# The output projections with seven block products for eight

## The chip, the cores and the metric

One core of a Trainium2 chip runs one program. The metric is the device time of one execution in microseconds (us), lower is better. The kernel before was timed in three runs.

## The reference, cut to what matters

The reference runs a first block (a mixer of three branches and a feed-forward layer) and then two layers of a second block (attention and a recurrent branch side by side). Three places multiply a concatenated activation by a 1024 x 1024 output weight and add the gated product to the residual stream. All is fp32.

```python
# first block: called "one" here; x has 1024 tokens
y_lat = jnp.concatenate([hy_lat, gla_lat, gdn_lat], axis=-1) @ w_out
x = x + g1 * y
x = x + g2 * sq_relu_mlp(modulate(x, norm2_g[l], sh2, sc2), w_mlp1[l], w_mlp2[l])
...
# second block, l = 0 ("two0") and l = 1 ("two1")
out_x = jnp.concatenate([att_x, m_x], axis=-1) @ w_out
x = x + gate_x * out_x
if not last:                       # two0 alone: 256 more tokens
    out_c = jnp.concatenate([att_c, m_c], axis=-1) @ w_out
    ctx = ctx + gate_c * out_c
```

After "one" and "two0" comes a root-mean-square norm with scale and shift, whose result feeds the next matrix products. After "two1" comes the final norm and the output.

## The kernel before, in words

**Storage.** Activations lie channel-major: channel in the partition, tokens along the free dimension, 8 channel tiles of 128. `XT` is the residual stream, `cat` the concatenated activation, `hT0` (region `R1`) the normed stream. Token blocks (`BLKS`) are 512, 512 and 256 (context) tokens. Weights come through a ring of four 1 MB slots (`K.W`), each with 256 output channels of the weight, that is one pair of output tiles.

**Stages.** The program is a list of stages (`plan`), and each engine's instructions are written out stage by stage in that order. Semaphores order the engines; `begin` makes an engine wait for what every engine did last in the stage before. Within a stage each engine works its own list in order, so an instruction that waits holds all behind it.

**Output projection** (`OutProj`, line 3213, three instances). TensorE walks the blocks, in each of them the 8 output tiles, and in each tile 8 matmuls over the inner channel tiles (L3247) into one of six PSUM banks. An fp32 matmul of the program is two MATMUL records in the trace. For each tile VectorE adds gate times product to `XT` (L3268), ScalarE squares the sum (L718), GpSimd adds the squares up (L728). "one" and "two1" have two blocks, "two0" three.

**The norm that follows** (`Rms`, line 825; `Finish` in "two1") is cut into parts 0 to 7 for each block. In part 1 TensorE multiplies the sum of squares by the mean matrix (L735, L737). In part 2 ScalarE takes Ln (L902) out of bank 6 and Exp (L904), each with a load of its table. In parts 3 to 7 VectorE scales eight tiles (L888) and ScalarE shifts them (L908). The projection runs the parts of block i - 1 one by one behind the tiles of block i; the parts of the last block come after the projection. In `Finish` part 1 is a small mean product (L3635) and Ln and Exp (L3653, L3656); parts 2 to 5 transpose four token tiles each (L3644), of which the block 0 ones use banks 6 and 7 alone; VectorE and ScalarE scale them (L3675, L3661), GpSimd multiplies by the gain (L3688), and SyncE stores them (L3712).

**Around the projections.** In "one" the residual stream comes back from HBM by a 4 MB DMA that GpSimd issues when the stage before has ended (`RestoreX`, L3198); VectorE waits for it ahead of its first add. Then GpSimd fetches two tiles of the second block's context. Behind "one" TensorE works in this order: mean product of block 1, the transposes of those two context tiles into banks 4, 5, 7 and 6 (L779), and the feed-forward layer (L3423). In "two0" and "two1" the stream is fetched during attention (L4738), and all projection weights but the first slot wait until attention's last transposes. Behind "two0" TensorE begins with the gate rows of block 0 (L1095), each matmul of which waits for the normed tile it reads.

**Seven for eight, as the feed-forward layer has it** (`Mlp.seven`, L3376). A 2 x 2 by 2 x 2 block product is made of seven block products instead of eight, with four sums of weight quarters on GpSimd (L3499 to L3505) and sums of input quarters on VectorE (L3517 to L3523 for its first product). Three products accumulate in bank "a", which is read out in between:

```python
product(a, S2, T2, False).then_inc(P.sem, P.up(("mlp", "P16", a)))
pr.open(e, d)
product(d, S1, T1, True).then_inc(P.sem, P.up(("mlp", "P5", d)))
```

## Time and profile before

| what | value |
| --- | --- |
| runs | 3688.92, 3693.72 and 3693.81 us; median 3693.72 us |
| profiled execution | span 3689.8 us; its own time is not listed apart from the span |
| mean granted TensorE clock | 0.988 of full speed |
| TensorE matmul busy | 3569.2 us, 97% |
| VectorE, ScalarE, GpSimd busy | 47%, 26%, 17% |
| all three output projections (L3247) | 896 MATMUL records |

The span runs from the first to the last instruction of one profiled execution; the runs' times include what lies around it. Matmuls are pipelined, so a record's duration overlaps the next one; the step from one tile's end to the next is the time that counts. "issue" is time for which the profile shows nothing that was waited for. TensorE's granted clock has two levels, 1.2 and 2.4 GHz, given as 0.5 and 1.0; a window's figure is the mean over it.

### The profile page before, as it was taken

How to read it: one execution, taken by the hardware profiler on the slowest of the kernel's cores; microseconds unless marked ns; L12 is line 12 of the kernel's file. 1: busy time of each engine (PE TensorE's matmuls, PEld its weight loads, DVE VectorE, ACT ScalarE, POOL GpSimd, SP SyncE). 2: the span in 40 equal slices, each digit the busy share in tenths (PEclk: the TensorE clock that was granted, in tenths of full speed). 3: DMA queues.
4: the chain of work that ended last, by engine and by line, in shares of the span. 5: the costliest groups of instructions: out<-in, count | busy, mean ns of one | idle time of the engine just before them, and what ended most of it. 6: DMA issues, size and time to landing. Idle time of an engine off the chain costs nothing.

```text
span 3689.8 us, 48255 instructions
## 1 busy us (share of the span) xinstructions
PE 3569.2 (97%) x19396; PEld 2260.5 (61%) x19396; DVE 1726.9 (47%) x3669; ACT 972.1 (26%) x1822; POOL 629.7 (17%) x572
## 2 busy tenths in 40 slices
PE   6999999999989999999999999999999999999998
PEld 3578976754744444444444588867654568866654
DVE  3877873274752334344334836323531464523531
ACT  5224422222103100000015214313541312313531
POOL 4002220231001312222214013110001102211001
PEclk8999999999989999999999999999999999999999
DMA  6301130453351111111102214120020413210021
GB/s 203 143 10 35 38 112 19 147 198 107 135 187 46 46 35 45 46 46 46 46 25 90 93 61 113 33 72 12 1 92 0 173 36 94 79 61 24 1 86 46
DMA packets 190445, 266.05 MB, mean 72 GB/s; under 512 B 27309, under 2 KB 133400, under 8 KB 189584
## 3 DMA queue, kind: packets, MB, share of 16 engines
q1 hardware_dynamic: 176576, 194.70, 16.9%
q0 software_dynamic: 13648, 68.26, 4.9%
q8 instruction: 157, 2.57, 0.3%
q14 instruction: 64, 0.52, 0.0%
HBM read 228.11 MB, written 34.81 MB: 71 GB/s over the span
## 4 chain that ended last, share of the span: by engine, by line
PE 88%; DVE 5%; ACT 2%; issue 2%; DMA 1%; POOL 0%; POOLq 0%; SPq 0%; DVEq 0%; ACTq 0%
PE ps L3376 19%; PE ps L3247 9%; PE ps L1038 9%; PE ps L4338 7%; PE ps L1060 6%; PE ps L4631 4%; PE ps L4808 3%; PE ps L1125 2%; PE ps L4288 2%; PE ps L4865 2%; PE ps L4848 2%; PE ps L3444 1%; PE ps L2939 1%; PE ps L1817 1%; PE ps L1833 1%
## 5 line engine op out<-in xcount | busy, mean ns | idle before, releaser
L3376 PE MATMUL ps<-big 128*128 128x512 f32 x1624 | 697.1, 593 | 0.0
L3376 PEld LDWEIGHTS ps<-big 128*128 128x128 f32 x1624 | 309.1, 190 | 387.8 <-issue 384.7
L1038 PE MATMUL ps<-big 128*128 128x512 f32 (+1 forms) x1056 | 402.0, 541 | 0.0
L3247 PE MATMUL ps<-big 128*128 128x512 f32 (+1 forms) x896 | 361.0, 564 | 4.6 <-issue 2.6
L1038 PEld LDWEIGHTS ps<-big 128*128 128x128 f32 x1056 | 199.9, 190 | 195.9 <-issue 189.8
L3247 PEld LDWEIGHTS ps<-big 128*128 128x128 f32 x896 | 170.6, 191 | 190.0 <-issue 184.4
L3569 DVE SCALAR_TENSOR_TENSOR big<-ps,big 128x512 f32<-128x512 f32 x212 | 159.2, 751 | 242.6 <-PE ps L3376 208.6
L4338 PE MATMUL ps<-big 128*128 128x256 f32 x1152 | 252.6, 380 | 0.0
L4338 PEld LDWEIGHTS ps<-big 128*128 128x128 f32 x1152 | 217.6, 190 | 28.9 <-issue 0.7
L1060 PE MATMUL ps<-big 128*128 128x256 f32 (+1 forms) x1344 | 229.0, 333 | 0.0
L1060 PEld LDWEIGHTS ps<-big 128*128 128x128 f32 x1344 | 208.3, 191 | 21.9 <-ACT big L2342 2.5
L3268 DVE SCALAR_TENSOR_TENSOR big<-ps,big 128x512 f32<-128x512 f32 (+1 forms) x56 | 39.8, 712 | 315.1 <-PE ps L3247 295.1
L728 POOL TENSOR_TENSOR big<-big 128x512 f32<-128x512 f32 (+1 forms) x90 | 109.5, 1222 | 439.8 <-ACT big L718 437.8
L718 ACT ACTIVATE big<-big 128x512 f32<-128x512 f32 (+1 forms) x120 | 68.5, 594 | 393.4 <-DVE big L3268 312.0
L1207 DVE SCALAR_TENSOR_TENSOR big<-big 128x1024 f32<-128x1024 f32 x130 | 168.8, 1299 | 4.6
L4631 PE MATMUL ps<-big 128*128 128x512 f32 (+1 forms) x416 | 158.5, 544 | 1.9 <-DVE big L4522 1.9
L4959 DVE CUSTOM_DVE_ANT_0 big<-ps,big 128x512 f32<-128x512 f32 (+2 forms) x144 | 96.0, 705 | 133.6 <-PE ps L4836 127.4
L4808 PE MATMUL ps<-big 128*128 128x256 f32 x576 | 132.5, 384 | 0.0
L3559 DVE TENSOR_TENSOR big<-big,ps 128x512 f32<-128x512 f32 x45 | 30.8, 685 | 213.6 <-PE ps L3376 213.6
L1125 PE MATMUL ps<-big 128*128 128x512 f32 (+1 forms) x320 | 126.7, 553 | 3.0 <-ACT big L1185 2.0
L4631 PEld LDWEIGHTS ps<-big 128*128 128x128 f32 x416 | 79.0, 190 | 80.6 <-issue 75.9
L4808 PEld LDWEIGHTS ps<-big 128*128 128x128 f32 x576 | 106.7, 190 | 26.9 <-DVE big L4963 9.7
(516 smaller groups left out, 5245.6 us busy)
## 6 DMA issues: line engine op xcount, KB each, us to landing
big<-in_w_mlp SPq DMA_DIRECT2D x32, 1024.0 KB, 5.4
big<-in_w_in SPq DMA_DIRECT2D x29, 1024.0 KB, 5.6
big<-in_w_mod SPq DMA_DIRECT2D x24, 1024.0 KB, 7.4
big<-in_w_ada SPq DMA_DIRECT2D x24, 1024.0 KB, 5.6
big<-us_scratch SPq DMA_DIRECT2D x72, 256.0 KB, 4.5
hs_scratch<-big POOLq DMA_DIRECT2D x3, 5120.0 KB, 19.0
xs_scratch<-big POOLq DMA_DIRECT2D x16, 640.0 KB, 3.5
big<-hs_scratch POOLq DMA_DIRECT2D x9, 1024.0 KB, 8.1
```

Source lines behind the costliest of these rows:

```text
L728: e.tensor_tensor(self.acc[i], self.acc[i], self.sq[q % len(self.sq)][:, 0:n], ALU.add).then_inc(G.sem, G.up(("added", self.tag, q), ("sum ...
L1038: t = e.matmul(b[:, 0:n], wv[:, k, 128 * m:128 * m + 128], K.hT[:, k, t0:t0 + n], start=(k == 0), stop=(k == 7))
L1060: t = e.matmul(b[:, 0:nn], K.hT[:, k, 128 * i:128 * i + 128], wv[:, k, 0:nn], start=(k == 0), stop=(k == 7))
L1125: t = e.matmul(b[:, 0:n], wv[:, k, 128 * m:128 * m + 128], K.hT[:, k, t0:t0 + n], start=(k == 0), stop=(k == 7))
L1207: e.scalar_tensor_tensor(dlat, zlat[:, :, tap:tap + c.seg], c.wcol(m, tap), dlat, ALU.mult, ALU.add).then_inc(V.sem, V.up((self.tag, c.wha ...
L3247: t = e.matmul(b[:, 0:n], wv[:, k, c:c + 128], cat[:, k, t0:t0 + n], start=(k == 0), stop=(k == 7))
L3376: t = e.matmul(z, w[:, k, c], y, start=(first and k == 0), stop=(k == nk - 1), skip_group_check=not first)
L3569: e.scalar_tensor_tensor(x, self.bank(u)[:, :], self.gcol[:, c:c + 1], x, ALU.mult, ALU.add).then_inc(V.sem, V.up(*keys))
L4338: x = e.matmul(b[:, 256 * q:256 * q + 256], m.hT[:, k, 128 * t:128 * t + 128], wv[:, k, :], start=(k == 0), stop=(k == 7))
L4631: t = e.matmul(b[:, 0:n], wv[:, k, c:c + 128], K.hT[:, k, t0:t0 + n], start=(k == 0), stop=(k == 7))
L4808: t = e.matmul(b[:, 0:256], wv[:, k, 128 * (j % 2):128 * (j % 2) + 128], K.hT[:, k, 256 * p:256 * p + 256], start=(k == 0), stop=(k == 7))
L4959: e.tensor_tensor_reduce(S[c][:, c0:512], self.s.bank(u)[:, c0:512], m.wm[:, c0:512], 64 ** -0.5, (m.m0 if n < 7 else m.snk)[:, c:c + 1], ...
```

## The change

The 1024 x 1024 by 1024 x 1024 product is cut into pairs of output tiles. One pair is a 2 x 2 by 2 x 2 block product: 2 output tiles x 2 halves of the inner channels x 2 blocks of 512 tokens. It is now made with seven products of 4 matmuls each, 28 matmuls for 32. "two0" does this for all four pairs and then the 256 context tokens directly; "one" and "two1" do it for three pairs, and the last pair (tiles 6 and 7, both blocks) directly.

New work: four subtractions of 128 x 2048 on VectorE at each projection's start (`input_sums`), ahead of the wait for the residual stream and of the first add; four sums of 128 x 512 on GpSimd for each pair (`weight_sums`), those of two pairs ahead of the first sum of squares; and seven adds into `XT` for a pair instead of four (`seven_out`). The T sums lie in `R1`, the S sums in its end and in spare memory. The squares follow the new order of tiles (`made`). The norm's parts move: in "two0" the parts of blocks 0 and 1 both run behind the eight context tiles, n-th parts behind the n-th tile, with the mean products in banks 6 and 7; in "one" and "two1" parts 0 to 2 of block 0 run behind tile (block 1, 6) and parts 3 to 7 behind the last tile, (block 1, 7).

```diff
@@ -703,15 +703,17 @@
-    def __init__(self, K, tag, x, blks, at_ring, at_sums, ring=3, g=None):
+    def __init__(self, K, tag, x, blks, at_ring, at_sums, ring=3, g=None, order=None):
         self.at, self.mean = K.book.at, K.mean
+        order = [(i, k) for i in range(len(blks)) for k in range(8)] if order is None else order
+        self.number = {x: q for q, x in enumerate(x for x in order if 0 < x[1] < 7)}
         self.tag, self.x, self.blks, self.g = tag, x, blks, g
...
-        q, ring = 6 * i + k - 1, len(self.sq)
+        q, ring = self.number.get((i, k), 0), len(self.sq)
...
-        q, n = 6 * i + k - 1, self.blks[i][1]
+        q, n = self.number[i, k], self.blks[i][1]
         e.wait_ge(*self.at("square", self.tag, i, k))
         if k > 1:
-            e.wait_ge(*self.at("added", self.tag, q - 1))
+            e.wait_ge(*self.at("added", self.tag, self.number[i, k - 1]))
...
-    def __init__(self, K, tag, w, gates, blks, after, sums, post, away=None, held=None):
...
-        self.cat = K.big[:, K.M0:K.M0 + 8 * (TT if len(blks) == 3 or tag != "one" else T)]
+        n = TT if len(blks) == 3 or tag != "one" else T
+        self.cat = K.big[:, K.M0:K.M0 + 8 * n].rearrange("p (a b) -> p a b", a=8)
+        self.sevens = self.pairs(blks)
+        self.ts = [K.R1[:, 2048 * i:2048 * i + 2048].rearrange("p (k t) -> p k t", k=4) for i in range(4)]
+        self.ws = [[mem.get(512).rearrange("p (k c) -> p k c", k=4) for _ in range(4)] for _ in range(2)]
+
+    @staticmethod
+    def pairs(blks):
+
+        return 4 if len(blks) == 3 else 3
+
+    @classmethod
+    def rest(cls, blks):
+
+        if len(blks) == 3:
+            return [(2, j) for j in range(8)]
+        return [(i, j) for i in range(2) for j in range(2 * cls.pairs(blks), 8)]
+
+    @classmethod
+    def made(cls, blks):
+
+        return [(i, 2 * p + m) for p in range(cls.pairs(blks)) for m in range(2) for i in range(2)] + cls.rest(blks)
+
+    def parts(self, n):
+
+        if len(self.blks) == 3:
+            return [(i, n) for i in range(2)]
+        return {2: [(0, j) for j in range(3)], 3: [(0, j) for j in range(3, 8)]}.get(n, [])
+
+    def direct(self):
+
+        for n, (i, j) in enumerate(self.rest(self.blks)):
+            t0, w = self.blks[i]
+            yield n, i, t0, w, j, (self.tag, "out", j, t0)
+
+    def key(self, p, x):
+        return (self.tag, "seven", p, x)
+
+    def ready(self, i, j):
+
+        if (i, j) in self.rest(self.blks):
+            return self.at("free", (self.tag, "out", j, self.blks[i][0]), 0)
+        p = j // 2
+        if i == 0:
+            return self.at("free", self.key(p, "a" if j % 2 else "b"), 0)
+        return self.at(self.tag, "P167 out", p) if j % 2 else self.at("free", self.key(p, "d"), 0)
...
-    def steps(self):
-        for i, (t0, n) in enumerate(self.blks):
-            for j in range(8):
...
+    def quarters(self, wv):
+        return [[wv[:, 4 * j:4 * j + 4, 128 * i:128 * i + 128] for j in range(2)] for i in range(2)]
+
+    def blocks(self):
+        return [[self.cat[:, 4 * j:4 * j + 4, 512 * i:512 * i + 512] for i in range(2)] for j in range(2)]
+    def seven(self, e, P, pr, p, wv, used):
+
+        a, b, d = (self.key(p, x) for x in "abd")
+        W, X, (T1, T2, T3, T4), (S1, S2, S3, S4) = self.quarters(wv), self.blocks(), self.ts, self.ws[p % 2]
+        bank = {}
+
+        def product(u, w, x, first=False):
+            for k in range(4):
+                t = e.matmul(bank[u][:, :], w[:, k, :], x[:, k, :], start=(first and k == 0), stop=(k == 3),
+                             skip_group_check=not first)
+            return t
+
+        bank[a] = pr.open(e, a)
+        product(a, W[0][0], X[0][0], True).then_inc(P.sem, P.up((self.tag, "P1", p)))
+        bank[b] = pr.open(e, b)
+        product(b, W[0][1], X[1][0], True).then_inc(P.sem, P.up(("mm", b)))
+        e.wait_ge(*self.at(self.tag, "weight sum", p, 2))
+        e.wait_ge(*self.at(self.tag, "input sum", 2))
+        e.wait_ge(*self.at(self.tag, "P1 out", p))
+        product(a, S2, T2).then_inc(P.sem, P.up((self.tag, "P16", p)))
+        bank[d] = pr.open(e, d)
+        product(d, S1, T1, True).then_inc(P.sem, P.up((self.tag, "P5", p)))
+        e.wait_ge(*self.at(self.tag, "weight sum", p, 3))
+        e.wait_ge(*self.at(self.tag, "input sum", 3))
+        e.wait_ge(*self.at(self.tag, "P16 out", p))
+        product(a, S3, T3).then_inc(P.sem, P.up((self.tag, "P167", p)))
+        e.wait_ge(*self.at(self.tag, "weight sum", p, 4))
+        e.wait_ge(*self.at(self.tag, "P5 out", p))
+        product(d, S4, X[1][1]).then_inc(P.sem, P.up(("mm", d)))
+        e.wait_ge(*self.at(self.tag, "input sum", 4))
+        e.wait_ge(*self.at(self.tag, "P167 out", p))
+        product(a, W[1][1], T4).then_inc(P.sem, P.up(("mm", a), (self.tag, "sums used", p), used))
 
     def tensor(self, e):
         K, P = self.K, self.sig("tensor")
         self.begin(e)
-        pr = Banks(K, range(6))
-        cat = self.cat.rearrange("p (a b) -> p a b", a=8)
         ws = []
-        for i, t0, n, j, u in self.steps():
-            if i == 0 and j % 2 == 0:
+        for p in range(self.sevens):
+            ws.append(K.W.use(e, 256))
+            self.seven(e, P, pr, p, ws[p][1], ws[p][0])
+        for n, i, t0, w, j, u in self.direct():
+            if len(ws) == j // 2:
                 ws.append(K.W.use(e, 256))
             used, wv = ws[j // 2]
             b = pr.open(e, u)
...
-                t = e.matmul(b[:, 0:n], wv[:, k, c:c + 128], cat[:, k, t0:t0 + n], start=(k == 0), stop=(k == 7))
+                t = e.matmul(b[:, 0:w], wv[:, k, c:c + 128], self.cat[:, k, t0:t0 + w], start=(k == 0), stop=(k == 7))
             t.then_inc(P.sem, P.up(("mm", u), used))
-            if i:
-                self.post.tensor_part(e, i - 1, j)
+            for x in self.parts(n):
+                self.post.tensor_part(e, *x)
 
     def scalar(self, e):
         S = self.sig("scalar")
         self.begin(e)
-        for i, t0, n, j, u in self.steps():
-            e.wait_ge(*self.at("free", u, 0))
+        n = 0
+        for i, j in self.made(self.blks):
+            e.wait_ge(*self.ready(i, j))
             self.sums.square(e, S, i, j)
+            if (i, j) in self.rest(self.blks):
+                for x in self.parts(n):
+                    self.post.scalar_part(e, *x)
+                n += 1
+
...
+    def add(self, e, V, mm, u, i, j, *keys):
+
+        (t0, n), gate = self.blks[i], self.gates[1 if i == 2 else 0]
+        x = self.K.XT[:, j, t0:t0 + n]
+        e.wait_ge(*self.at(*mm))
+        e.wait_ge(V.sem, V.n)
+        e.scalar_tensor_tensor(x, self.bank(u)[:, 0:n], gate[:, j:j + 1], x, ALU.mult, ALU.add).then_inc(V.sem, V.up(*keys))
+
+    def input_sums(self, e, V):
+
+        X, (T1, T2, T3, T4) = self.blocks(), self.ts
+        e.tensor_tensor(T1, X[0][1], X[0][0], ALU.subtract).then_inc(V.sem, V.up())
+        e.wait_ge(V.sem, V.n)
+        e.tensor_tensor(T2, X[1][1], T1, ALU.subtract).then_inc(V.sem, V.up((self.tag, "input sum", 2)))
+        e.tensor_tensor(T3, X[1][1], X[0][1], ALU.subtract).then_inc(V.sem, V.up((self.tag, "input sum", 3)))
+        e.wait_ge(*self.at(self.tag, "input sum", 2))
+        e.tensor_tensor(T4, X[1][0], T2, ALU.subtract).then_inc(V.sem, V.up((self.tag, "input sum", 4)))
+
+    def seven_out(self, e, V, p):
+
+        a, b, d = (self.key(p, x) for x in "abd")
+        c, t = 2 * p, self.tag
+        self.add(e, V, (t, "P1", p), a, 0, c, (t, "P1 out", p))
+        self.add(e, V, ("mm", b), b, 0, c, ("free", b, 0))
+        self.add(e, V, (t, "P16", p), a, 1, c, (t, "P16 out", p))
+        self.add(e, V, (t, "P5", p), d, 1, c + 1, (t, "P5 out", p))
+        self.add(e, V, (t, "P167", p), a, 1, c + 1, (t, "P167 out", p))
+        self.add(e, V, ("mm", d), d, 1, c, ("free", d, 0))
+        self.add(e, V, ("mm", a), a, 0, c + 1, ("free", a, 0))
 
...
         self.begin(e)
+        self.input_sums(e, V)
         e.wait_ge(*self.at("x back", self.tag))
-        for i, t0, n, j, u in self.steps():
...
+        for p in range(self.sevens):
+            self.seven_out(e, V, p)
+        for n, i, t0, w, j, u in self.direct():
+            self.add(e, V, ("mm", u), u, i, j, ("free", u, 0))
+            for x in self.parts(n):
+                self.post.vector_part(e, *x)
+
+    def weight_sums(self, e, G, p, u):
+
+        W = self.quarters(self.K.W.slots[u % len(self.K.W.slots)].rearrange("p (k c) -> p k c", k=8))
+        S1, S2, S3, S4 = self.ws[p % 2]
+        e.wait_ge(*self.at("weights", "in", u))
+        if p >= 2:
+            e.wait_ge(*self.at(self.tag, "sums used", p - 2))
+        e.tensor_tensor(S1, W[1][0], W[1][1], ALU.add).then_inc(G.sem, G.up())
+        e.wait_ge(G.sem, G.n)
+        e.tensor_tensor(S2, S1, W[0][0], ALU.subtract).then_inc(G.sem, G.up((self.tag, "weight sum", p, 2)))
+        e.tensor_tensor(S3, W[0][0], W[1][0], ALU.subtract).then_inc(G.sem, G.up((self.tag, "weight sum", p, 3)))
+        e.wait_ge(*self.at(self.tag, "weight sum", p, 2))
+        e.tensor_tensor(S4, W[0][1], S2, ALU.subtract).then_inc(G.sem, G.up((self.tag, "weight sum", p, 4)))
...
-        for i, t0, n, j, u in self.steps():
+        u = self.base
+        for p in range(2):
+            self.weight_sums(e, G, p, u + p)
+        n = 0
+        for i, j in self.made(self.blks):
             self.sums.add(e, G, i, j)
-            if i:
-                self.post.gpsimd_part(e, i - 1, j)
-            if self.away is not None and i == len(self.blks) - 1:
+            if (i, j) not in self.rest(self.blks):
+                p = j // 2 + 2
+                if j % 2 and i and p < self.sevens:
+                    self.weight_sums(e, G, p, u + p)
+                continue
+            for x in self.parts(n):
+                self.post.gpsimd_part(e, *x)
+            n += 1
...
+    sums = Sums(K, "rms2", K.XT, BLKS[0:2], tmp, tmp, order=OutProj.made(BLKS[0:2]))
...
+    mem = Arenas([Arena(K.big, K.total - 2048, K.total), tmp])
+    yield OutProj(K, "one", A["w_out"][0], (K.m6(2), None), BLKS[0:2], "hyena", sums, rms, mem)
...
+        sums = Sums(K, f"rms{5 + l}", K.XT, blks, tmp, tmp, order=OutProj.made(blks))
...
+            post.own = (6, 7, 6)
+            mem = Arenas([Arena(K.big, K.total - 2048, K.total), tmp])
...
+            post, mem = Finish(K, sums, A["final_g_2"]), tmp
```

## Rows read from the trace of the kernel before

**Rows 1.** The page: the chain that ended last, by engine and by line.
```profile
PE 88%; DVE 5%; ACT 2%; issue 2%; DMA 1%; POOL 0%; POOLq 0%; SPq 0%; DVEq 0%; ACTq 0%
PE ps L3376 19%; PE ps L3247 9%; PE ps L1038 9%; PE ps L4338 7%; PE ps L1060 6%; PE ps L4631 4%; PE ps L4808 3%; PE ps L1125 2%; PE ps L4288 2%; PE ps L4865 2%; PE ps L4848 2%; PE ps L3444 1%; PE ps L2939 1%; PE ps L1817 1%; PE ps L1833 1%
```
**Rows 2.** Groups by line, forms apart: busy us, mean ns, idle before, releasers.
```profile
L3247 PE MATMUL ps<-big 128*128 128x512 f32 x768 | 333.2, 595 | 4.6 <-issue 2.6 <-DVE big L4995 2.0
```
**Rows 3.** Timeline, projection "one": start us, us, engine line op out<-in xcount [idle before].
```profile
1111.24 0.75 DVE L3268 SCALAR_TENSOR_TENSOR big<-ps,big 128x512 f32<-128x512 f32 x1 [6.12 <-PE ps L3247]
...
1118.10 0.75 DVE L3268 SCALAR_TENSOR_TENSOR big<-ps,big 128x512 f32<-128x512 f32 x1 [6.12 <-PE ps L3247]
```
**Rows 4.** Timeline, feed-forward stage: the same copy of two neighbouring seven-product sets.
```profile
1238.03 0.60 ACT L3478 ACTIVATE big<-ps 128x512 f32<-128x512 f32 x1 [9.70 <-PE ps L3376]
...
1262.07 0.60 ACT L3478 ACTIVATE big<-ps 128x512 f32<-128x512 f32 x1 [9.70 <-PE ps L3376]
```
**Rows 5.** Timeline, start of projection "one": TensorE, the reload of x, the first add.
```profile
1068.10 70.56 PE L3247 MATMUL ps<-big 128*128 128x512 f32 x160 [2.62 <-issue]
1068.54 0.89 POOL L3198 DMA_DIRECT2D big<-xs_scratch  x1 [135.11 <-ACT big L3049]
...
1083.97 1.41 DVE L3268 SCALAR_TENSOR_TENSOR big<-ps,big 128x512 f32<-128x512 f32 x2 [19.95 <-DMA big<-xs_scratch]
```
**Rows 6.** Windows around pauses of TensorE: length, busy by engine, then granted clock (PEclk).
```profile
1068.10:1074.90 6.80, 6.80 (x12) 3.00 (x13) 0.00 (x0) 0.00 (x0) 1.97 (x3) 0.75 0.66 231
...
1052.00:1058.00 6.00, 6.00 (x15) 4.67 (x15) 2.51 (x3) 0.00 (x0) 0.00 (x0) 0.52 1.09 349
```
**Rows 7.** Groups by line, forms apart: subtractions on VectorE; weight sums on GpSimd.
```profile
L3101 DVE TENSOR_TENSOR big<-big 128x1024 f32<-128x1024 f32 x4 | 4.9, 1219 | 0.0
...
L3521 DVE TENSOR_TENSOR big<-big 128x2048 f32<-128x2048 f32 x1 | 3.2, 3236 | 0.0
...
L3523 DVE TENSOR_TENSOR big<-big 128x2048 f32<-128x2048 f32 x1 | 2.7, 2747 | 1.8 <-PE ps L3423 1.8
...
L3499 POOL TENSOR_TENSOR big<-big 128x512 f32<-128x512 f32 x29 | 36.8, 1268 | 502.5 <-PE ps L3376 502.5
```
**Rows 8.** Timeline, starts of projections "two0" and "two1".
```profile
2748.18 0.69 DVE L4995 TENSOR_TENSOR big<-ps,big 128x512 f32<-128x512 f32 x1 [0.18 <-PE ps L4878]
2749.08 51.31 PE L3247 MATMUL ps<-big 128*128 128x512 f32 x119 [1.01 <-DVE big L4995]
...
3558.70 68.91 PE L3247 MATMUL ps<-big 128*128 128x512 f32 x160 [1.01 <-DVE big L4995]
```
**Rows 9.** Timeline, end of projection "one".
```profile
1181.62 0.75 DVE L3268 SCALAR_TENSOR_TENSOR big<-ps,big 128x512 f32<-128x512 f32 x1 [5.46 <-PE ps L3247]
...
1183.80 1.28 ACT L902 ACT_TABLE_LOAD   x1
...
1185.10 0.69 ACT L902 ACTIVATE big<-ps,big 128x512 f32<-128x512 f32 x1
...
1185.84 0.66 PE L779 MATMUL ps<-big 128*128 128x128 f32 x4 [0.31 <-ACT big L902]
...
1188.62 5.36 ACT L908 ACTIVATE big<-big 128x512 f32<-128x512 f32 x8 [0.89 <-DVE big L888]
```
**Rows 10.** Timeline, end of projection "two0".
```profile
2888.01 0.72 ACT L908 ACTIVATE big<-big 128x512 f32<-128x512 f32 x1 [0.24 <-DVE big L888]
...
2890.80 0.42 ACT L718 ACTIVATE big<-big 128x256 f32<-128x256 f32 x1 [2.07 <-DVE big L3268]
...
2891.02 1.92 PE L1095 MATMUL ps<-big 128*32 128x512 f32 x16 [0.78 <-DVE big L3268]
```
**Rows 11.** Timeline, end of projection "two1".
```profile
3636.10 1.04 PE L3644 MATMUL ps<-big 128*128 128x128 f32 x8
...
3674.14 0.75 DVE L3268 SCALAR_TENSOR_TENSOR big<-ps,big 128x512 f32<-128x512 f32 x1 [6.12 <-PE ps L3247]
...
3679.23 0.20 ACT L3656 ACTIVATE big<-big 128x4 f32<-128x4 f32 x1
```

More of the change, by code:

```diff
@@ L3213, with __init__ @@
 class OutProj(Stage):
-    def __init__(self, K, tag, w, gates, blks, after, sums, post, away=None, held=None):
+    def __init__(self, K, tag, w, gates, blks, after, sums, post, mem, away=None, held=None):
         super().__init__(K, "out_proj", tag, after)
@@ L3275, in gpsimd @@
         self.begin(e)
-        for i, t0, n, j, u in self.steps():
-            self.sums.add(e, G, i, j)
-            if i:
-                self.post.gpsimd_part(e, i - 1, j)
-            if self.away is not None and i == len(self.blks) - 1:
+        u = self.base
[3 more added lines that the diff above has]
+        for i, j in self.made(self.blks):
+            self.sums.add(e, G, i, j)
+            if (i, j) not in self.rest(self.blks):
[6 more added lines that the diff above has]
+            n += 1
+            if self.away is not None and i == 2:
                 X = self.lane(f"x{j}_away")
-                e.wait_ge(*self.at("free", u, 0))
+                e.wait_ge(*self.at("free", (self.tag, "out", j, self.blks[i][0]), 0))
                 e.dma_start(K.xs[:, j, :], K.XT[:, j, :]).then_inc(X.sem, X.up(("x away", self.away, j), by=16))
@@ L5215, in plan @@
     tmp = K.spare()
-    sums = Sums(K, "rms2", K.XT, BLKS[0:2], tmp, tmp)
+    sums = Sums(K, "rms2", K.XT, BLKS[0:2], tmp, tmp, order=OutProj.made(BLKS[0:2]))
     cols = (("quads1", "columns"), K.col("norm2_g", 0, 8), (K.m6(4), K.m6(3)), None)
     rms = Rms(K, "rms2", K.XT, K.hT0, BLKS[0:2], [(sums, i) for i in range(2)], tmp, cols, begun=1)
-    yield OutProj(K, "one", A["w_out"][0], (K.m6(2), None), BLKS[0:2], "hyena", sums, rms)
+    mem = Arenas([Arena(K.big, K.total - 2048, K.total), tmp])
+    yield OutProj(K, "one", A["w_out"][0], (K.m6(2), None), BLKS[0:2], "hyena", sums, rms, mem)
     yield rms
@@ L5245, in plan @@
         tmp, blks = K.spare(), BLKS if l == 0 else BLKS[0:2]
-        sums = Sums(K, f"rms{5 + l}", K.XT, blks, tmp, tmp)
+        sums = Sums(K, f"rms{5 + l}", K.XT, blks, tmp, tmp, order=OutProj.made(blks))
         if l == 0:
```

14 lines of the change are left out of this document (3 added, 11 removed).

## The prediction

> **What bounds the kernel now.** I read the page first, and on it the chain of waits that ended last: 88% of the span lies on TensorE, and line 3247, the output projections, holds 9% [rows 1]. So a matmul taken away is worth its full step, and a pause of TensorE costs its full length. The grouped lines give 768 records of 512 columns, 384 matmuls of the program, with 4.6 us idle before them in all [rows 2]: today nothing is waited for inside a projection. The timeline gives the step: in steady state VectorE's adds of two tiles start 6.86 us apart [rows 3], so one matmul of 512 columns takes 6.86 / 8 = 0.858 us. The 595 ns of a record overlap with its neighbour and are not used.
>
> **What is saved.** Ten pairs (3 + 4 + 3) lose 4 matmuls each: 40 x 0.858 = 34.3 us. Seven products in a row keep this pace: in the feed-forward layer the same copy of two neighbouring sets starts 24.04 us apart, and 28 x 0.858 is 24.02 [rows 4]. The seven adds of a pair take 7 x 0.75 = 5.3 us of VectorE and the four weight sums 4 x 1.27 = 5.1 us of GpSimd [rows 3, 7], beside 24 us of TensorE. Sums of the third and fourth pair are queued a whole pair ahead. Inside and between pairs I cost nothing: every read-out has another product of 3.43 us as cover. Without that cover it would be 0.75 us an add. No DMA is added, and GpSimd's reload and context fetches stay ahead of the new sums in its list. The first squares are added up behind eight weight sums; ScalarE waits for that with its ring of three, TensorE for neither.
>
> **Start of "one".** The two products that need no sums end at 1068.10 + 6.87 us, plus 1.7 for the clock. That 1.7 comes from the window: 6.80 us at a clock of 0.75 are 1.7 us of lost work, after a pause of 2.62 us [rows 5, 6]. This part is in the time before too. So they end at 1076.7. The third product accumulates into bank "a" after the first was read out, and this add stands behind the reload of x, which lets VectorE go at 1083.97 [rows 5]. Before, six banks covered this; now two products do. TensorE goes on at 1083.97 + 0.75 + 0.1 = 1084.8: **8.1 us** of pause. The four subtractions are done by then (1068.1 + 4 x 3.24 = 1081.1). The reload is issued while VectorE subtracts, which no row prices; between 0 and 3 us, I take 0 because the issue itself is only 0.89 us [rows 5].
>
> **Starts of "two0" and "two1".** Here x is there, and the subtractions end last. A 128 x 2048 subtraction beside GpSimd's sums took 3.24 us, another one that overlapped them in part 2.75, and half the size alone 1.22 [rows 7]. GpSimd has eight sums queued, which are more than 13 us when slowed, so all four run beside it: 4 x 3.24 = 13.0; the lower end is 8 x 1.22 = 9.8. I take 13.0. In "two0" VectorE is free at 2748.87, so the first add is done at 2748.9 + 13.0 + 0.75 + 0.1 = 2762.7; TensorE has done its two products at 2749.08 + 6.87 = 2755.95 [rows 8]. That is **6.7 us** of pause (3.5 at the lower end), and the same in "two1": twice.
>
> **The clock behind these pauses.** After the 2.62 us pause 1.7 us were lost; some 16 us earlier the clock stood at 0.52 through 6.00 us of unbroken matmuls, 2.9 us lost [rows 5, 6]. The 1.01 us pauses left the next tile whole [rows 8]. My pauses are of 6.7 to 8.1 us; I take 1.7 each, the row of the same line and shape (ends 1.0 and 3.1) and three of them: **5.1 us**.
>
> **End of "one".** Call the end of the last matmul E. Before, E was 1181.6, ScalarE went straight from the last square to block 1's table load, and Ln ended at E + 4.2, which freed bank 6 for the last four context transposes; then the feed-forward layer began [rows 9]. Now the eight scalings and shifts of block 0 stand between: scaling from E + 0.75, shifts end at about E + 6.9 (eight take 5.36 us), then 1.28 of table load and 0.69 of Ln: E + 8.9 [rows 9]. TensorE waits **4.7 us** longer. This pause also comes before dense matmuls: **1.7 us** for the clock (ends 0 and 3.1). Block 1's normed tiles come some 5 us later than before, but the first two feed-forward tiles (13.7 us) still cover them.
>
> **End of "two0".** Both blocks' parts now share eight tiles of 256 tokens, 3.43 us each, with two mean products of 1.72 us behind the second: E is 30.9 us after the first begins. The third is done at 13.7, its square at 14.7. Then ScalarE has two Ln and two Exp with four table loads, 4 x 1.28 + 4 x 0.69 = 7.9 us [rows 9]: 22.6. Then five squares of 0.42 and 15 shifts of 0.72 up to the last one of block 0, 12.9 us [rows 10]: 35.5, that is E + 4.6. The gate rows wait for it and end about there plus 0.1. Before, they began 0.78 us after E and took 1.92 [rows 10]. So 4.7 for 2.7 us: **2 us**, and 1 for a clock that may fall in this trickle, **3.0** (0.5 to 5).
>
> **End of "two1".** Transposes of three token tiles, 3 x 0.87 us, move from among the tiles [rows 11] to behind E: E is 2.6 us earlier. They share banks 6 and 7 and step at the pace of ScalarE's copies, so that block 1's Exp ends about 8.5 us after E instead of 5.3 [rows 11]. Behind tile (1, 6) the first transposes wait 1.3 us for the Ln that frees bank 6. Sum 3.2 + 1.3 - 2.6 = **1.9 us** (0 to 4). The stores of block 0 are out before those of block 1 begin.
>
> **The sum.** Costs: 8.1 + 2 x 6.7 + 5.1 + 4.7 + 1.7 + 3.0 + 1.9 = 37.9 us. Against 34.3 saved: **3.6 us slower**. The profiled execution shows only its span, 3689.8 us; the median of the runs, 3693.72, lies 3.9 above, which I take as what lies around a span. The forecast is 3693.7 + 3.6 = 3697.3 us, 0.1% more. A measurement of this kernel can tell about 0.2%, 7.4 us, from no change.
>
> **Rivals.**
> *The clock decides, slower.* Place: four restarts before dense matmuls (three starts, the end of "one"). If each costs the 3.1 us that the longer low stretch suggests (6.00 us at 0.52 and what came just before) instead of 1.7, the sum is 3.6 + 4 x 1.4 = 9.2: 3702.9 us. It decides from 2.65 us a restart. For it: my pauses are two to three times the one of 2.62 us. Against it: the row of the same line [rows 6]. The Trainium skill (TensorE: Matmul & The Clock Gate, HAM oscillation) says that a long enough wait between two bursts of matmuls throttles the engine again, at every burst anew; by it none of the four is spared, and the two windows agree.
> *The sums are quick, faster.* If the subtractions take 1.22 us per 1024 columns, each of the two pauses is 3.1 us shorter (the ends above, rounded), 6.2 in all; if the clock then holds there and at the end of "one", 3 x 1.7 = 5.1 more are kept: 3.6 - 11.3 = -7.7, 3686.0 us. Against it: the 3.24 us row is the same shape with the same neighbour [rows 7]. The Trainium skill (GPSIMD Engine Reference, 8. Key points) says that GpSimd shares its SBUF interfaces with VectorE and contends with instructions of two SBUF inputs, which these are; by it this rival fails, and the 3.24 against twice 1.22 agrees.
> *The change does not bring its saving*, if a read-out holds every product: then none of the 34.3 is saved, 3731.6 us. The 24.04 us speak against it [rows 4].
>
> **How the numbers follow.** The waits eat the gain: 0.50, with 3690 to 3701 as its own range. The clock, or a late reload, puts it above 7.4 us: 0.33. Quick sums: 0.15. No saving: 0.02. So faster 0.15, same 0.50, slower 0.35. The range reaches from the quick sums (3686) to both the clock rival and about 4 us more of the open ends, the reload's 3 among them (3707).
>
> **What would show it.** Right: 816 records of the projections' matmuls instead of 896 (10 x 8 fewer), the first add of "one" right at the reload's end, a TensorE pause of 8 us there and of about 6.7 us in the other two, subtractions of 3.2 us, Ln of block 1 about 9 us behind the last add in "one", and a granted clock of 0.5 behind each pause. Wrong: no pause behind the second product; subtractions of 2.4 us; a pause inside later pairs; block 1's scalings late for the feed-forward layer's third tile.

## The result, and the profile after

Over 20 runs of each kernel the median went from 3693.59 to **3700.75 us**: a ratio of 1.0019, 95% interval 1.0013 to 1.0025, so 5 to 9 us slower. The forecast was 3697.3. The measured median lies at the upper edge of the likeliest case's own range (3690 to 3701), and its 7.2 us lie so close to the 7.4 at which the prediction's slower case begins that the interval reaches past it. The profiled execution of after has a span of 3698.6 us.

The page of after, the chain that ended last: TensorE's share fell from 88 to 87%, VectorE's rose from 5 to 7 [rows 1]; the seven products (L3290) and the direct ones (L3330) share what L3247 held.

```profile
PE 87%; DVE 7%; ACT 3%; issue 2%; DMA 2%; POOL 0%; DVEq 0%; SPq 0%; POOLq 0%; ACTq 0%
PE ps L3516 19%; PE ps L1040 9%; PE ps L4478 7%; PE ps L1062 6%; PE ps L3290 6%; PE ps L4771 4%; PE ps L4948 3%; PE ps L1127 2%; PE ps L4428 2%; PE ps L3330 2%; PE ps L5005 2%; PE ps L4988 2%; PE ps L3584 1%; PE ps L2941 1%; PE ps L1819 1%
```

The groups by line of after, forms apart (busy us, mean ns of one, idle before). L3361 is the third input subtraction, L3401 the fourth weight sum:

```profile
L3290 PE MATMUL ps<-big 128*128 128x512 f32 x560 | 248.5, 606 | 24.7 <-DVE big L3353 20.0 <-issue 2.6 <-DVE big L5135 2.0
L3330 PE MATMUL ps<-big 128*128 128x512 f32 x128 | 55.6, 592 | 0.0
L3330 PE MATMUL ps<-big 128*128 128x256 f32 x128 | 28.0, 379 | 0.0
...
L3401 POOL TENSOR_TENSOR big<-big 128x512 f32<-128x512 f32 x10 | 18.8, 1880 | 0.0
L3361 DVE TENSOR_TENSOR big<-big 128x2048 f32<-128x2048 f32 x3 | 10.0, 3350 | 0.0
```

560 + 128 + 128 = 816 records: the multiplications did go. Before the first group stand 20.0 us of idle time that were not there [rows 2], all from VectorE's adds (L3353). The waits of after (us in all, times, longest) show that for the seven products this is three waits and nothing else, and a new wait of the context transposes (L781):

```profile
PE ps L3290 <- DVE big L3353: 20.0, 3, 8.0
...
PE ps L781 <- ACT big L904: 5.0, 1, 5.0
```

The timeline of after at the start of "one". It answers to [rows 5]: TensorE stops at 1077.9, the reload of x lets the first add go at 1085.01, and TensorE goes on after 8.00 us:

```profile
1070.81 7.11 PE L3290 MATMUL ps<-big 128*128 128x512 f32 x16 [2.63 <-issue]
1071.25 0.89 POOL L3200 DMA_DIRECT2D big<-xs_scratch  x1 [132.82 <-ACT big L3051]
...
1073.13 3.55 DVE L3360 TENSOR_TENSOR big<-big 128x2048 f32<-128x2048 f32 x1
1073.23 1.28 POOL L3396 TENSOR_TENSOR big<-big 128x512 f32<-128x512 f32 x1
...
1085.01 1.61 DVE L3353 SCALAR_TENSOR_TENSOR big<-ps,big 128x512 f32<-128x512 f32 x2 [1.80 <-DMA big<-xs_scratch]
...
1085.91 14.49 PE L3290 MATMUL ps<-big 128*128 128x512 f32 x29 [8.00 <-DVE big L3353]
...
1091.43 0.75 DVE L3353 SCALAR_TENSOR_TENSOR big<-ps,big 128x512 f32<-128x512 f32 x1 [4.81 <-PE ps L3290]
1094.86 0.75 DVE L3353 SCALAR_TENSOR_TENSOR big<-ps,big 128x512 f32<-128x512 f32 x1 [2.68 <-PE ps L3290]
```

From the restart (1085.91) to the next add are 5.52 us; in the pace of full clock the adds are 3.43 apart, as 1091.43 and 1094.86 are. The same view at the start of "two0" answers to [rows 8]:

```profile
2757.75 2.29 DVE L3358 TENSOR_TENSOR big<-big 128x2048 f32<-128x2048 f32 x1 [0.20 <-DVE big L5135]
2757.76 7.11 PE L3290 MATMUL ps<-big 128*128 128x512 f32 x16 [1.02 <-DVE big L5135]
2757.79 3.38 POOL L3396 TENSOR_TENSOR big<-big 128x512 f32<-128x512 f32 x1 [18.94 <-issue]
2760.08 3.24 DVE L3360 TENSOR_TENSOR big<-big 128x2048 f32<-128x2048 f32 x1
...
2766.51 3.35 DVE L3363 TENSOR_TENSOR big<-big 128x2048 f32<-128x2048 f32 x1
...
2769.99 1.60 DVE L3353 SCALAR_TENSOR_TENSOR big<-ps,big 128x512 f32<-128x512 f32 x2
2770.89 14.67 PE L3290 MATMUL ps<-big 128*128 128x512 f32 x28 [6.02 <-DVE big L3353]
...
2777.01 0.75 DVE L3353 SCALAR_TENSOR_TENSOR big<-ps,big 128x512 f32<-128x512 f32 x1 [5.42 <-PE ps L3290]
```

The add stands right behind the fourth subtraction, with no idle time: the subtractions hold TensorE for 6.02 us. "two1" shows the same 6.02. Windows of 6.80 us of after (length, busy by engine, then the granted clock) behind the three pauses and behind the one at the end of "one", as in [rows 6]:

```profile
1085.91:1092.71 6.80, 6.80 (x12) 3.06 (x13) 1.46 (x2) 0.63 (x1) 3.44 (x3) 0.73 0.07 28
2770.89:2777.69 6.80, 6.80 (x11) 2.94 (x12) 1.38 (x2) 0.63 (x1) 5.03 (x5) 0.64 0.00 0
3579.73:3586.53 6.80, 6.80 (x10) 2.90 (x11) 1.33 (x2) 0.63 (x1) 5.03 (x5) 0.63 0.00 0
1192.23:1199.03 6.80, 6.80 (x14) 2.95 (x14) 5.71 (x9) 5.90 (x10) 0.00 (x0) 0.77 0.01 2
```

A mean of 0.64 over 6.80 us is time spent at the lower level (1.2 GHz, 0.5 of full) and then at the upper; (1 - 0.64) x 6.80 = 2.4 us of work lost. The four lost 1.8, 2.4, 2.5 and 1.6. The same windows of after's second trace (1080.47, 2765.95, 3573.50 and 1187.47 us) have 0.63, 0.58, 0.73 and 0.72: 2.5, 2.9, 1.8 and 1.9.

The end of "one" of after, answering to [rows 9]. Eight scalings and eight shifts stand ahead of block 1's table load and Ln (L904), and the last transposes wait 4.95 us for it:

```profile
1182.47 0.75 DVE L3353 SCALAR_TENSOR_TENSOR big<-ps,big 128x512 f32<-128x512 f32 x1 [7.73 <-PE ps L3330]
...
1183.91 5.36 ACT L910 ACTIVATE big<-big 128x512 f32<-128x512 f32 x8
...
1189.29 1.28 ACT L904 ACT_TABLE_LOAD   x1
1190.59 0.69 ACT L904 ACTIVATE big<-ps,big 128x512 f32<-128x512 f32 x1
...
1191.33 1.12 PE L781 MATMUL ps<-big 128*128 128x128 f32 x4 [4.95 <-ACT big L904]
```

The end of "two0" of after, answering to [rows 10], and then of "two1", to [rows 11]. The gate rows (L1097) begin as the last direct tile ends, at 2893.86, and their last four records wait for shifts:

```profile
2893.79 1.91 PE L1097 MATMUL ps<-big 128*32 128x512 f32 x12
...
2897.30 1.38 ACT L910 ACTIVATE big<-big 128x512 f32<-128x512 f32 x2
2898.07 1.05 PE L1097 MATMUL ps<-big 128*32 128x512 f32 x2 [0.75 <-ACT big L910]
...
3679.35 0.75 DVE L3353 SCALAR_TENSOR_TENSOR big<-ps,big 128x512 f32<-128x512 f32 x1 [5.70 <-PE ps L3330]
...
3686.23 5.36 PE L3784 MATMUL ps<-big 128*128 128x128 f32 x32
...
3687.98 0.20 ACT L3796 ACTIVATE big<-big 128x4 f32<-128x4 f32 x1
```

**A ledger of stretches.** One span is a poor yardstick here: the first matmul of "one" started between 1065.1 and 1073.6 us in the traces below, before anything that the kernels do differently. So every comparison of traces uses stretches, each the difference of two starts in the timeline: "one" from its first matmul to the first seven-product matmul of the feed-forward layer, "two0" from its first matmul to the mean product of block 2, "two1" from its first matmul to the end of the span, and the two stretches between them, whose code the change leaves alone. The last column is the median against before on the same chip.

```
kernel                  one    between    two0   between    two1   the three  ratio [95% interval]
before               145.70    1535.28  144.33    665.29  131.10      421.13
before, again        145.69    1535.28  144.33    665.29  131.11      421.13  1.0001 [0.9992, 1.001]
after                150.46    1536.49  141.83    667.01  132.00      424.29  1.0019 [1.0013, 1.0025]
after, again         151.72    1535.97  142.26    665.30  131.32      425.30  1.002  [1.0011, 1.0029]
late subtractions    150.73    1536.65  133.14    665.30  124.90      408.77  0.9971 [0.9959, 0.9983]
bank 3               143.47    1536.82  141.85    667.00  132.00      417.32  0.9992 [0.9983, 1.0]
matmuls in the pause 151.26    1536.26  139.43    666.97  131.24      421.93  1.0002 [0.9994, 1.0011]
"one" as before      144.05    1536.10  141.93    667.27  131.94      417.92  0.9996 [0.9987, 1.0004]
no weight sums       150.48    1535.51  136.33    666.99  128.08      414.89  0.9992 [0.9983, 1.0]
direct tiles first   141.71    1535.59  142.29    665.28  124.55      408.55  0.9962 [0.9949, 0.9974]
late + bank 3        143.35    1536.86  133.15    665.27  124.93      401.43  0.9959 [0.9945, 0.9972]
all three            133.26    1535.86  133.15    666.97  124.82      391.23  0.9929 [0.9917, 0.9941]
```

Against before, after's trace is +4.8 in "one", -2.5 in "two0", +0.9 in "two1": +3.2 us, and +2.9 between them. The rest of its 8.8 us of span is the start (1070.8 against 1068.1).

### The profile page after: what moved, and what is told of

It reads as the page before. It is cut to its first block, busy times and chain, and to the rows that moved or that the text cites. A ratio compares the mean times of both kernels' runs of the same rounds, so it can differ in the third digit from the quotient of the medians.

```text
span 3698.6 us, 48302 instructions
## 1 busy us (share of the span) xinstructions
PE 3548.4 (96%) x19316; PEld 2247.6 (61%) x19316; DVE 1786.5 (48%) x3711; ACT 970.4 (26%) x1822; POOL 699.7 (19%) x612
## 3 DMA queue, kind: packets, MB, share of 16 engines
q1 hardware_dynamic: 176576, 194.70, 16.7%
## 4 chain that ended last, share of the span: by engine, by line
PE 87%; DVE 7%; ACT 3%; issue 2%; DMA 2%; POOL 0%; DVEq 0%; SPq 0%; POOLq 0%; ACTq 0%
PE ps L3516 19%; PE ps L1040 9%; PE ps L4478 7%; PE ps L1062 6%; PE ps L3290 6%; PE ps L4771 4%; PE ps L4948 3%; PE ps L1127 2%; PE ps L4428 2%; PE ps L3330 2%; PE ps L5005 2%; PE ps L4988 2%; PE ps L3584 1%; PE ps L2941 1%; PE ps L1819 1%
## 5 line engine op out<-in xcount | busy, mean ns | idle before, releaser
L3516 PE MATMUL ps<-big 128*128 128x512 f32 x1624 | 697.1, 592 | 0.0
L3516 PEld LDWEIGHTS ps<-big 128*128 128x128 f32 x1624 | 308.6, 190 | 388.4 <-issue 385.3
L1040 PE MATMUL ps<-big 128*128 128x512 f32 (+1 forms) x1056 | 403.4, 542 | 0.0
L1040 PEld LDWEIGHTS ps<-big 128*128 128x128 f32 x1056 | 200.1, 191 | 197.1 <-issue 190.7
L3290 PE MATMUL ps<-big 128*128 128x512 f32 x560 | 248.5, 606 | 24.7 <-DVE big L3353 20.0
L4478 PEld LDWEIGHTS ps<-big 128*128 128x128 f32 x1152 | 217.2, 190 | 29.3 <-issue 0.7
L1062 PEld LDWEIGHTS ps<-big 128*128 128x128 f32 x1344 | 208.0, 191 | 22.2 <-ACT big L2344 2.5
L3290 PEld LDWEIGHTS ps<-big 128*128 128x128 f32 x560 | 108.5, 195 | 162.9 <-issue 151.7
L3353 DVE SCALAR_TENSOR_TENSOR big<-ps,big 128x512 f32<-128x512 f32 (+1 forms) x86 | 62.4, 725 | 246.7 <-PE ps L3290 179.3
L4771 PE MATMUL ps<-big 128*128 128x512 f32 (+1 forms) x416 | 161.8, 552 | 1.9 <-DVE big L4662 1.9
L3639 POOL TENSOR_TENSOR big<-big 128x512 f32<-128x512 f32 x29 | 36.8, 1270 | 504.3 <-PE ps L3516 504.2
L4771 PEld LDWEIGHTS ps<-big 128*128 128x128 f32 x416 | 80.1, 193 | 82.8 <-issue 78.1
L1127 PE MATMUL ps<-big 128*128 128x512 f32 (+1 forms) x320 | 126.7, 552 | 3.0 <-ACT big L1187 2.0
```

The source lines that it names most:

```text
L1040: t = e.matmul(b[:, 0:n], wv[:, k, 128 * m:128 * m + 128], K.hT[:, k, t0:t0 + n], start=(k == 0), stop=(k == 7))
L1062: t = e.matmul(b[:, 0:nn], K.hT[:, k, 128 * i:128 * i + 128], wv[:, k, 0:nn], start=(k == 0), stop=(k == 7))
L1127: t = e.matmul(b[:, 0:n], wv[:, k, 128 * m:128 * m + 128], K.hT[:, k, t0:t0 + n], start=(k == 0), stop=(k == 7))
L3290: t = e.matmul(bank[u][:, :], w[:, k, :], x[:, k, :], start=(first and k == 0), stop=(k == 3), skip_group_check=not first)
L3516: t = e.matmul(z, w[:, k, c], y, start=(first and k == 0), stop=(k == nk - 1), skip_group_check=not first)
L4478: x = e.matmul(b[:, 256 * q:256 * q + 256], m.hT[:, k, 128 * t:128 * t + 128], wv[:, k, :], start=(k == 0), stop=(k == 7))
```

## The experiments

Both kernels ran once more, unchanged. Before:

> The kernel before once more, for a second trace of it. Both theories: equal to itself within 0.1%. Theory (waits): the three projection stretches repeat within 2 us, while the start of the first projection shifts by some us with the clock's low stretches before it. Rival (elsewhere): that start is again 2.7 us earlier than in the changed kernel's traces.

After:

> The changed kernel once more, nothing edited, for a second trace. Theory (waits): the stretch from the start of each projection to the next stage's steady work repeats within 2 us: about +4.8 us in "one", -2.5 in "two0", +0.9 in "two1" against before; what lies outside of these stretches (5.6 us in the first pair of traces) is drift of the clock's low stretches and changes from run to run, so the time is 3 to 7 us above before. Rival (elsewhere): a fixed cost outside of the projections shows again, in the same stages and with the same size.

Before repeated its three stretches to 0.01 us. After showed the pauses again (6.61, 6.03 and 6.03 us) and +4.2 us over the three stretches. In "one" its first two products ran at a mean clock of 0.76 and took 8.74 us instead of 7.11; the pause behind them was shorter by 1.4 us, since the reload of x ends it, and TensorE went on 15.34 us after its start, 15.10 in the first trace. So a slow clock ahead of that pause costs next to nothing.

**Late subtractions.** The third and fourth subtraction go behind the first and third add of pair 0:

```
-        e.tensor_tensor(T3, X[1][1], X[0][1], ALU.subtract)...     (in input_sums, T4 likewise)
 ...
         self.add(e, V, (t, "P1", p), a, 0, c, (t, "P1 out", p))
+        if p == 0:
+            self.late_sum(e, V, 3)
         self.add(e, V, ("mm", b), b, 0, c, ("free", b, 0))
         self.add(e, V, (t, "P16", p), a, 1, c, (t, "P16 out", p))
+        if p == 0:
+            self.late_sum(e, V, 4)
```

> The third and fourth subtraction of VectorE move behind the first and the third add of the first pair. Theory (waits): in two0 and two1 the pause of 6.0 us falls below 1 us and the low clock behind it (about 2 us each) goes; "one" keeps its 8 us, since x is late there. 14 to 16 us faster than the changed kernel, so 7 to 9 us faster than before. Rival (clock only): the waits move to the fourth product and less than 5 us are won. Rival (elsewhere): under 10 us.

Both pauses went. The timeline of this kernel at the start of "two0":

```profile
2756.56 28.99 PE L3290 MATMUL ps<-big 128*128 128x512 f32 x67 [1.02 <-DVE big L5145]
...
2758.88 3.24 DVE L3360 TENSOR_TENSOR big<-big 128x2048 f32<-128x2048 f32 x1
...
2762.25 0.75 DVE L3353 SCALAR_TENSOR_TENSOR big<-ps,big 128x512 f32<-128x512 f32 x1
...
2762.91 2.48 DVE L3366 TENSOR_TENSOR big<-big 128x2048 f32<-128x2048 f32 x1
```

"two0" is 8.7 us shorter than in after, 6.02 of pause and 2.5 of slow clock among them. "two1" gained 7.1: its last direct tile took 8.40 us instead of 7.03, the clock's share given back elsewhere. "one" is as it was: there the reload holds the add, not the subtractions. Moving two subtractions a few instructions later was worth 0.5% of this kernel (ratios 1.002 and 0.9971), 15.9 us between the medians.

**Bank 3.** The context transposes of block 1 get another PSUM bank for their last quarter:

```
-        pr = Banks(self.K, (4, 5, 7, 6))
+        pr = Banks(self.K, (4, 5, 7, 3))
```

> The last four context transposes go to bank 3 instead of bank 6. Theory (waits): TensorE no longer waits 4.95 us for the Ln behind "one" and the feed-forward layer starts at full clock: 5 to 7 us faster than the changed kernel, about equal to before. Rival (norm late): the feed-forward layer's third tile then waits for block 1's normed tiles, and under 3 us are won.

The timeline at the end of "one" shows the sixteen transposes in one row and the feed-forward layer right behind them, four microseconds ahead of Ln:

```profile
1183.42 1.91 PE L781 MATMUL ps<-big 128*128 128x128 f32 x16
1185.16 27.63 PE L3563 MATMUL ps<-big 128*128 128x512 f32 x64
...
1189.10 0.69 ACT L904 ACTIVATE big<-ps,big 128x512 f32<-128x512 f32 x1
```

"one" took 7.0 us less. The 64 matmuls (L3563) took 29.20 us in after's trace, 27.63 here: with the pause went 1.6 us of slow clock. What TensorE had waited for was not Ln's result but the bank that Ln reads. The median fell by 8.3 us on the same chip, more than the 5 to 7 expected.

**Matmuls in the pause.** Behind the first two products of each projection 6 (in "one" 8) matmuls into the free bank 7, whose result nobody reads:

```
+        if p == 0:
+            for _ in range(8 if self.tag == "one" else 6):
+                e.matmul(self.K.psum[7][:, :], W[0][0][:, 0, :], X[0][0][:, 0, :], start=True, stop=True)
```

> Six matmuls (eight in "one") of a weight tile into the unused bank 7 fill the pause behind the second product of each projection; they add nothing to the result. Theory (clock costs about 2 us at each of three restarts): the third product takes 3.43 us instead of 5.5 and the time falls by 4 to 6 us against the changed kernel. Rival (the clock costs nothing, or the fill lengthens the pause): within 2 us of the changed kernel or slower.

The timeline of "two0" (L3300 are the additional matmuls, L3356 the adds):

```profile
2763.11 5.31 PE L3300 MATMUL ps<-big 128*128 128x512 f32 x12
...
2769.30 16.12 PE L3290 MATMUL ps<-big 128*128 128x512 f32 x37 [0.88 <-DVE big L3356]
...
2773.01 0.75 DVE L3356 SCALAR_TENSOR_TENSOR big<-ps,big 128x512 f32<-128x512 f32 x1 [3.00 <-PE ps L3290]
```

The product behind the pause now comes to its add after 3.71 us instead of 6.12, with the same subtractions ahead. That is the clock's part alone: 2.4 us, and "two0" is 2.4 shorter. In "one" the next add came 3.71 us behind the restart too (5.52 in after), but the reload of x took longer in this trace, 15.6 us from its issue to the first add instead of 13.8, so "one" as a whole gained nothing; "two1" gained 0.8. The median is 5.9 us below that of after.

**"one" as before.** Only "two0" and "two1" use seven products:

```
-    yield OutProj(K, "one", A["w_out"][0], (K.m6(2), None), BLKS[0:2], "hyena", sums, rms, mem)
+    yield OutProj(K, "one", A["w_out"][0], (K.m6(2), None), tuple(BLKS[0:2]), "hyena", sums, rms, mem)
 ...
     def pairs(blks):
+        if isinstance(blks, tuple):
+            return 0
```

> "one" multiplies directly as before, "two0" and "two1" keep the seven products. Theory (waits): "one" alone makes the change slower, by 4.8 to 6 us: the time is 4 to 7 us below the changed kernel, within 3 us of before. Rival (all three lose alike): a third of the loss goes, 1 to 3 us.

"one" took 144.05 us, 6.4 less than after's with both starting at full clock, and the ratio fell to 0.9996: the change made "one" slower, and in the other two it brought next to nothing.

**No weight sums.** This kernel leaves GpSimd's weight sums out and multiplies plain quarters of the weights in their place, so its output is not the reference's. The subtractions stay, and lose only their neighbour:

```
+        S1, S2, S3, S4 = W[1][0], W[0][1], W[1][1], W[0][0]
 ...
-        for p in range(2):
-            self.weight_sums(e, G, p, u + p)
```

> GpSimd makes no weight sums; TensorE multiplies with the plain weight quarters in their place, so the projections' results are left out. Theory (VectorE's subtractions are slowed by GpSimd beside them): the second to fourth take 2.3 us instead of 3.24 to 3.35, the pause in two0 and two1 falls from 6.0 to about 3 us, 6 to 8 us faster than the changed kernel. Rival (they are slow by themselves, by their operands): they stay at 3.2 us and the time stays within 2 us.

The timeline of "two0", and the windows behind its pause and behind that of "two1":

```profile
2752.09 2.29 DVE L3356 TENSOR_TENSOR big<-big 128x2048 f32<-128x2048 f32 x1 [0.20 <-DVE big L5127]
...
2758.83 2.28 DVE L3361 TENSOR_TENSOR big<-big 128x2048 f32<-128x2048 f32 x1
...
2762.15 18.26 PE L3291 MATMUL ps<-big 128*128 128x512 f32 x42 [2.94 <-DVE big L3351]
```
```profile
2762.15:2768.95 6.80, 6.80 (x16) 3.11 (x17) 1.46 (x2) 0.63 (x1) 0.00 (x0) 1.00 0.00 0
3565.47:3572.27 6.80, 6.80 (x12) 2.95 (x13) 1.46 (x2) 0.63 (x1) 0.00 (x0) 0.75 0.00 0
```

All four subtractions take 2.28 or 2.29 us (two of them stand above), and the pause falls from 6.02 to 2.94. The neighbour costs 3.1 us here. In "two0" the clock stays at 1.00 behind the shorter pause: together 5.5 us, which is what the ledger shows. In "two1" the pause is 2.94 us too, but the clock behind it is 0.75: of the 2.5 us of slow clock behind the long pause only 0.8 come back, and "two1" is 3.9 us shorter. The median is 2.1 us below before's.

**Direct tiles first.** In "one" and "two1" block 0's two direct tiles run ahead of the seven products. Their weights are loaded twice, and the attention layer's memory moves on by one slot for that:

```
-        for j in range(0, 8, 2):
+        for q, j in enumerate((6, 0, 2, 4, 6) if self.head else (0, 2, 4, 6)):
 ...
+            for n, i, t0, w, j, u in rest[0:2]:
+                b = pr.open(e, u)
+                for k in range(8):
 ...
-        m = AttMem(K, m.hT, (l + 2) % 4)
+        m = AttMem(K, m.hT, (l + 3) % 4)
```

> In "one" and "two1" the direct tiles 6 and 7 of block 0 are made first, ahead of the pairs (one weight slot is loaded twice for it). Theory (waits): 13.7 us of cover ahead of the first pair hide the reload of x in "one" (8.2 us and 2 for the clock) and the subtractions in "two1" (6.0 and 1.8): 17 to 19 us faster than the changed kernel, 10 to 12 faster than before. Rival (the wait moves on to another product or to the extra load): under 10 us.

The timeline at the start of "one" (L3328 direct, L3291 seven products, L3364 adds) has no pause left:

```profile
1069.08 15.55 PE L3328 MATMUL ps<-big 128*128 128x512 f32 x32 [2.64 <-issue]
...
1083.54 0.75 DVE L3364 SCALAR_TENSOR_TENSOR big<-ps,big 128x512 f32<-128x512 f32 x1 [2.06 <-DMA big<-xs_scratch]
...
1084.46 10.89 PE L3291 MATMUL ps<-big 128*128 128x512 f32 x25
```

"one" is 8.7 us shorter than after's (8.3 of them are 8.00 of pause and 1.9 of clock less the 1.6 by which its first products were slower), "two1" 7.4. The additional load cost nothing that shows. "two0", which has no such tiles, kept its 6.0 us of pause. The median is 13.4 us below before's, more than the 10 to 12 expected.

**All three, and the first two.** Each edit takes a different wait away, so if my account is right they add up.

> The three edits that each took a wait away, together: two direct tiles of block 0 first in the projections of two blocks, T3 and T4 subtracted behind the first and third add, block 1's context transposes in bank 3 instead of 6. My theory (the gain is the 34.3 us of matmuls and was given back at four places that hardly touch each other): 'one' takes about 134.7 us (141.7 with the direct tiles first, less the 7.0 that the other bank gave), 'two0' about 133.1, 'two1' about 124.5; together 392.3 against 421.1 of the kernel before, 28.8 us less, span near 3663, ratio about 0.9925. Rival (the waits stand behind one another: a pause taken away at the start only moves the wait to ScalarE's or VectorE's work at the end of the projection): 'one' stays at 138 or more, the three together above 398, ratio 0.994 or more.

> The late subtractions and bank 3 alone, with the pause of 8.0 us at the start of 'one' left in and no additional weight load. My theory: 'one' about 143.5, 'two0' about 133.1, 'two1' about 124.9; together 401.5 against 421.1 of the kernel before, 19.6 us less, ratio about 0.995; against the kernel with all three edits the difference is the pause in 'one' with its slow matmuls, 8 to 9 us. Rival (the pause in 'one' covers something that then has to be waited for later): the difference to the kernel with all three is under 4 us.

The three stretches took 391.23 us (392.3 expected) and 401.43 (401.5 expected). The difference of the two is 10.2 us, above the 8 to 9 expected: in the kernel without the direct tiles first, "one" still has a pause of 7.95 us with a clock of 0.72 behind it, 1.9 us more. With all three, "one" took 133.26 us, 1.4 less than expected, for its first products ran at full clock (13.97 us for 32 records, 15.55 in the kernel with the direct tiles alone). The median of late subtractions and bank 3 is 16.7 us below before's, where 19.6 were expected; 1.6 of the missing 2.9 are the stretch behind "one". The median of all three together is 3663.93 us against 3691.74 of before, **27.8 us faster**, ratio 0.9929 [0.9917, 0.9941]. The rival, that a wait taken away reappears behind it, is out. This version beats both kernels. Its timeline at the start of the seven products in "one":

```profile
1079.75 15.61 PE L3291 MATMUL ps<-big 128*128 128x512 f32 x36
...
1083.38 0.75 DVE L3364 SCALAR_TENSOR_TENSOR big<-ps,big 128x512 f32<-128x512 f32 x1 [1.40 <-PE ps L3291]
```

A product started at 1079.75 at full clock, and its add came 3.63 us later. Against this 3.63, the 5.52, 6.12 and 6.18 us behind after's three pauses (the last from 3579.73 to 3585.91) lost 1.9, 2.5 and 2.5 us.

## Why the prediction was right, step by step

The likeliest case came in: the waits ate the gain, each at the place given. All its terms have a measured counterpart in after's trace. That their sum came within 1 us is in part luck, since terms that were too large and too small cancel.

- **The saving, 34.3 us.** The pace held. From 1098.30 to 1146.36 after's adds are 14 steps of 3.43 us, two whole sets in 48.06. No wait stands inside or between pairs: the three waits above are all. And with the waits of all four places gone the stretches are 421.13 - 391.23 = 29.9 us shorter, so the saving was there to be had.
- **Start of "one", 8.1 us:** 8.00 measured, and for the reason given: the add went when the reload of x had landed. The open bound, a reload slowed by the subtractions, does not show: from issue to first add 13.8 us, 15.4 before [rows 5], and never over 15.6 in the traces behind it.
- **Starts of "two0" and "two1", 6.7 each:** 6.02. The step that was off is "4 x 3.24": all four ran beside GpSimd's sums, but the first was not slowed by that. It took 2.29 us, the other three 3.24 to 3.35.
- **The clock behind the pauses, 3 x 1.7 = 5.1 us:** 1.9 + 2.5 + 2.5 = 6.9. This term was sized too small; I had taken the row behind the 2.62 us pause, and a pause of 6 us cost more than that. The errors on the pauses of "two0" and "two1" (-1.4 together) and on the clock (+1.8) all but cancel.
- **End of "one", 4.7 + 1.7:** 4.95 less the 0.31 of before [rows 9] is 4.6, and 1.6 for the clock. Bank 3 gave both back.
- **End of "two0", 3.0:** "two0" changed by -2.5; less the 13.7 saved and with 6.0 and 2.5 at its start, 2.7 are left for the end. With E at 2893.86 the last gate rows, which wait for the last shift of block 0, began at 2898.07, E + 4.2 (4.6 predicted), and ended at 2899.12, E + 5.3, where they had ended at E + 2.7 before: 2.6 us. The 2 us of the chain were thus 2.6, and the 1 us for a falling clock has nothing behind it: no low stretch shows there.
- **End of "two1", 1.9:** by the same account 0.9 + 10.3 - 6.0 - 2.5 = 2.7. Block 1's Exp ended at E + 8.9 (8.5 predicted), but the last 32 transposes took 5.36 us instead of 3.69 in before's trace. A slow clock in this tail was not in my sum.
- **Not in the sum:** the stretches between were 2.9 us longer in after's trace and 0.7 in its second one, though the change does not touch their code. What they show of the clock stands in the last section.

In all +3.2 and +4.2 us over the three stretches where +3.6 was predicted. The medians differ by 7.2. The stretches between account for 1.8 of the missing 3.5 on average; the rest of about 2 us is within what the start of "one" shifts from trace to trace, and I could not place it.

**The rivals.** *The clock decides* needed 2.65 us a restart; the four took 1.9, 2.5, 2.5 and 1.6 in the first trace of after, and 2.3 on average in the second. It explains part of the difference from 3697.3, not the sign. What the Trainium skill (TensorE: Matmul & The Clock Gate, HAM oscillation) says of long waits between bursts held behind every pause of 6 us or more (0.58 to 0.74 in the 6.80 us behind it) and at the end of "one"; behind 2.94 us the clock fell in "two1" and held in "two0". *Quick sums* fell: three of the four subtractions were slowed, and the Trainium skill (GPSIMD Engine Reference, 8. Key points) names such instructions, with two SBUF inputs, as those that contend with GpSimd. Its price was right: without GpSimd's sums the pause was 3.1 us shorter, the size that this rival gave. *No saving* fell with the 3.43 us steps.

## What to carry to other kernels

Where an accumulator is read out and then written again, a step that saves matmuls shortens the cover of its own first read-out: list what VectorE has queued ahead of that first add, and leave ahead of it only what the very next product needs. Before pricing a late result, ask whether the waiter needs the result or only the buffer that its producer still reads: a different bank was worth 7.0 us. And run a few products that depend on nothing new first, as cover for a reload that is under way.
